# First products of a stage taken apart into those that need the rounded input and the one that needs its rest

## The reference

```python
def _ffn_half(h, g, shift, scale, gate, w_in, w_out):
    a, b = jnp.split(_modnorm(h, g, shift, scale) @ w_in, 2, axis=-1)
    return h + 0.5 * gate * ((jax.nn.silu(a) * b) @ w_out)
...
        u = rmsnorm(x, ln1_w[l])
        proj = u @ w_in[l]
...
        x = x + peer_ffn(rmsnorm(x, ln2_w[l]), peer_wq[l], peer_subkeys[l], peer_u[l], peer_v[l])
```

## Time and profile before

| | |
|---|---|
| median of 3 runs | 4942.17 us (4940.61 to 4943.07) |
| profiled execution, its own time | 4941.26 us |
| its span in the trace | 4939.4 us |
| mean granted TensorE clock | 0.937 |
| TensorE busy | 4507.5 us, 91% |
| GpSimd busy | 2803.5 us, 57% |
| ScalarE busy | 1752.6 us, 35% |
| VectorE busy | 1574.3 us, 32% |

### The profile page before, as it was taken

One profiled execution on the slowest core, in us unless ns is written; L12 is line 12 of the kernel. 1 busy time (PEld: TensorE's weight loads), 2 busy tenths in 40 slices (PEclk: granted clock), 3 DMA queues, 4 the chain that ended last, 5 costly groups with the idle time before them and its releaser, 6 DMA issues.

```text
span 4939.4 us, 72697 instructions
## 1 busy us (share of the span) xinstructions
PE 4507.5 (91%) x29978; PEld 4059.0 (82%) x29978; DVE 1574.3 (32%) x3005; ACT 1752.6 (35%) x2705; POOL 2803.5 (57%) x1354
## 2 busy tenths in 40 slices
PE   7998999999989898998867999999998866999999
PEld 5777777778878798977856999999977766999998
DVE  2211221031023232444578111112444678111112
ACT  3223322232143243441233444444441233444444
POOL 3343243344445276740467888887740467888886
PEclk9999999999999998988888999999987888999999
DMA  6624264222223144430130545545430130555544
GB/s 255 246 86 93 98 247 185 94 86 95 93 101 121 60 157 155 170 121 1 52 111 10 187 178 185 181 182 187 170 121 1 52 111 1 186 179 183 182 180 151
DMA packets 94371, 648.49 MB, mean 131 GB/s; under 512 B 9824, under 2 KB 16224, under 8 KB 16608
## 3 DMA queue, kind: packets, MB, share of 16 engines
q1 hardware_dynamic: 87120, 633.21, 34.9%
q10 hardware_dynamic: 7056, 12.49, 1.1%
HBM read 641.46 MB, written 4.19 MB: 131 GB/s over the span
## 4 chain that ended last, share of the span: by engine, by line
PE 83%; DVE 12%; ACT 2%; issue 1%; POOL 1%; DMA 1%; SPq 0%; DVEq 0%; ACTq 0%; POOLq 0%
PE ps L244 23%; PE ps L245 23%; PE ps L246 23%; PE ps L2529 3%; PE ps L399 1%; PE ps L1425 1%; PE ps L1456 1%; POOL ring_rest L260 1%; DVE arena L2091 1%; DVE x L746 1%; PE ps L1778 1%; PE ps L1825 1%; PE ps L988 1%; DMA arena<-in_mod_weights 1%; PE ps L1831 1%
## 5 line engine op out<-in xcount | busy, mean ns | idle before, releaser
L260 POOL TENSOR_TENSOR ring_rest<-ring,rounded 128x1024 fp32r<-128x1024 f32 x1032 | 2508.8, 2454 | 1621.1 <-ACT rounded L232 1353.0
L244 PE MATMUL ps<-part,rounded 128*128 128x256 f32 (+1 forms) x5760 | 1840.7, 320 | 104.5 <-DVE part L564 42.4
L245 PE MATMUL ps<-part,rounded 128*128 128x256 f32 (+1 forms) x5760 | 1828.4, 317 | 0.0
L246 PE MATMUL ps<-part,ring_rest 128*128 128x256 f32 (+1 forms) x5760 | 1826.4, 317 | 0.0
L244 PEld LDWEIGHTS ps<-part,rounded 128*128 128x128 f32 x5760 | 1112.5, 193 | 210.1 <-DVE part L564 40.7
L246 PEld LDWEIGHTS ps<-part,ring_rest 128*128 128x128 f32 x5760 | 1112.3, 193 | 69.2
L245 PEld LDWEIGHTS ps<-part,rounded 128*128 128x128 f32 x5760 | 1113.5, 193 | 66.8
L232 ACT ACTIVATE rounded<-ring 128x1024 fp32r<-128x1024 f32 x528 | 527.5, 1050 | 710.3 <-PE ps L246 702.8
L2651 ACT ACTIVATE rounded<-ring 128x1024 fp32r<-128x1024 f32 x504 | 531.5, 1055 | 378.8 <-DMA ring<-in_weights 371.7
L244 PE MATMUL ps<-x_parts,rounded 128*128 128x256 f32 x2304 | 654.9, 284 | 9.4 <-DVE x_parts L564 8.0
L245 PE MATMUL ps<-x_parts,rounded 128*128 128x256 f32 x2304 | 653.3, 284 | 0.0
(11 more groups left out here) (326 smaller groups left out, 4225.6 us busy)
## 6 DMA issues: line engine op xcount, KB each, us to landing
ring<-in_weights SPq DMA_DIRECT2D x528, 1024.0 KB, 4.8
arena<-in_mod_weights SPq DMA_DIRECT2D x72, 1024.0 KB, 7.8
arena<-bias_scratch ACTq DMA_DIRECT2D x2, 2048.0 KB, 9.2
bias_scratch<-arena ACTq DMA_DIRECT2D x1, 3072.0 KB, 32.1
x<-in_x SPq DMA_DIRECT2D x1, 2048.0 KB, 9.1
arena<-in_keys ACTq DMA_DIRECT2D x2, 1024.0 KB, 5.0
arena<-in_cst SPq DMA_DIRECT2D x1, 1216.0 KB, 29.7
arena<-in_expo ACTq DMA_DIRECT2D x1, 1024.0 KB, 5.0
```

The source lines that it names most:

```text
L244: mm(out, w[0], a[0], start=start, stop=False)
L245: mm(out, w[0], a[1], start=False, stop=False)
L246: return mm(out, w[1], a[0], start=False, stop=stop)
L260: eng.tensor_tensor(c.ring_rest[:, slot, half], c.ring[:, slot, half], c.rounded[:, (self.s0 + r) % ROUNDED, half].bitcast(F32), ALU.subtr ...
```

## The change

`product` is taken apart for the first products: `open_product` issues the two that read only the rounded input tile (w0·a0, w1·a0), `close_product` the one that reads the rest (w0·a1). For each feature tile TensorE waits for the rounded tile (`rounded_tile`, a wait on the norm's `rounded` count), issues the pairs of all open outputs, waits for the rest (`input_tile`) and issues the third products. The waits for the weights' rest stand in the first loop now, ahead of the pairs. In `PeerRoute` the bank number of the second output of block 0 moves from `part` into `first_queries`, unchanged. The sums are the same in another order.

```diff
--- before.py
+++ after.py
@@ -244,6 +244,21 @@
         mm(out, w[0], a[0], start=start, stop=False)
         mm(out, w[0], a[1], start=False, stop=False)
         return mm(out, w[1], a[0], start=False, stop=stop)
+
+    def open_product(self, out, w, a, start):
+
+        mm = self.nc.tensor.matmul
+        mm(out, w[0], a[0], start=start, stop=False)
+        mm(out, w[1], a[0], start=False, stop=False)
+
+    def close_product(self, out, w, a, stop):
+
+        return self.nc.tensor.matmul(out, w[0], a[1], start=False, stop=stop)
+
+    def rounded_tile(self, pe, k):
+
+        ready = self.before.rounded
+        pe.wait_ge(ready.sem, ready.at((k + 1) * self.before.t // N))
 
     def input_tile(self, pe, k):
 
@@ -630,12 +645,16 @@
             return last
 
         for k in range(KD // 2):
+            self.rounded_tile(pe, k)
+            outs = [(j, half, [w[:, half * KD + k, :] for w in self.weights(j)]) for j in range(2) for half in range(2)]
+            a = [u[:, k, :] for u in self.u]
+            for j, half, w in outs:
+                if k == 0:
+                    pe.wait_ge(c.rest_done[half], self.split_count(j))
+                self.open_product(c.ps[:, 2 * j + half, 0:self.t], w, a, k == 0)
             self.input_tile(pe, k)
-            for j in range(2):
-                for half in range(2):
-                    if k == 0:
-                        pe.wait_ge(c.rest_done[half], self.split_count(j))
-                    part(j, half, [k])
+            for j, half, w in outs:
+                self.close_product(c.ps[:, 2 * j + half, 0:self.t], w, a, False)
         for k in range(KD // 2, KD):
             self.input_tile(pe, k)
         for j in range(2):
@@ -1249,12 +1268,17 @@
             return last
 
         for k in range(KD // 2):
+            self.rounded_tile(pe, k)
+            outs = [(j, e, ps[:, self.bank(j, e), e * N:(e + 1) * N], [w[:, e * KD + k, :] for w in self.weights(j)])
+                    for j in range(2) for e in range(2)]
+            a = [u[:, k, :] for u in self.u]
+            for j, e, out, w in outs:
+                if k == 0:
+                    pe.wait_ge(c.rest_done[e], self.split_count(j))
+                self.open_product(out, w, a, k == 0)
             self.input_tile(pe, k)
-            for j in range(2):
-                for e in range(2):
-                    if k == 0:
-                        pe.wait_ge(c.rest_done[e], self.split_count(j))
-                    part(j, e, [k])
+            for j, e, out, w in outs:
+                self.close_product(out, w, a, False)
         for k in range(KD // 2, KD):
             self.input_tile(pe, k)
         for j in range(2):
@@ -2298,17 +2322,22 @@
             whi, wlo = self.weights(j)
             for k in tiles:
                 i = e * KD + k
-                last = self.product(ps[:, 3 if j == 0 and e else j % 2, e * N:(e + 1) * N], (whi[:, i, :], wlo[:, i, :]),
+                last = self.product(ps[:, j % 2, e * N:(e + 1) * N], (whi[:, i, :], wlo[:, i, :]),
                                     [z[:, k, :] for z in self.z], k == 0, k == KD - 1)
             return last
 
         def first_queries():
             for k in range(KD):
-                self.input_tile(pe, k)
-                for e in range(2):
+                self.rounded_tile(pe, k)
+                outs = [(e, ps[:, 3 * e, e * N:(e + 1) * N], [w[:, e * KD + k, :] for w in self.weights(0)]) for e in range(2)]
+                a = [z[:, k, :] for z in self.z]
+                for e, out, w in outs:
                     if k == 0:
                         pe.wait_ge(self.chip.rest_done[e], self.split_count(0))
-                    last = part(0, e, [k])
+                    self.open_product(out, w, a, k == 0)
+                self.input_tile(pe, k)
+                for e, out, w in outs:
+                    last = self.close_product(out, w, a, k == KD - 1)
             last.then_inc(self.chip.block_done, 1)
 
         def queries(j):
```

## The result

| | before | changed |
|---|---|---|
| median | 4941.49 us | 4951.08 us |
| runs, lowest to highest | 20, 4936.96 to 4943.32 | 20, 4947.58 to 4953.02 |
| ratio, 95% interval | | 1.0020 (1.0013 to 1.0026) |
| profiled execution, its span | 4941.26, 4939.4 us | 4947.58, 4945.8 us |

The change costs 9.6 us. The prediction said 4939.6 and a range to 4945: it was wrong, by 11.5 us, and the measured time lies 6.1 us above the range. The slowest run of before and the fastest run of the changed kernel are 4.3 us apart, so this isn't scatter. The profiled execution of the changed kernel is the fastest of its 20 runs: its trace accounts for 6.4 us of span, and what the other runs have more wasn't traced.

The account below looks back on a forecast made before the run. TensorE, busy 91% of the span, was taken as the bound, through its standstills and lower clock level. -2.64 - 1.38 + 1.50 = -2.52 us gave 4938.7 for the profiled execution, 4939.6 us as median; range 4935 to 4945.

Parts of the forecast that it names:

- Earlier starts: Three 512-token FeedForwardIn starts 0.88 us earlier each, two PeerRoute starts 0.69 us each: -2.64 and -1.38 us.
- The second block's wait: 256-token FeedForwardIn and both ProjectIn: late GpSimd weight rest leaves three third products behind the wait, 0.5 us each, 1.5 lost.
- Rises stay put or come early: Clock rises after cold starts: unmoved, gains halve, 4941.2 us, chance 0.24; or one spell sooner, 4937.5 us, chance 0.11.
- Exposed weight loads: Eight changed stages: new order needs one more 193 ns load for each of 128 products, +24.7 us, 4966.9; chance 0.01.
- What carries through: Stages behind the changed starts: the chain moves as a whole, so gains persist; in PeerRoute 0.69 us stays.
- The range: 4935 to 4945 us: early rises with one 3.3 us slow spell gained, to the slower case with one lost.
- something unseen: Leftover case without a named place or size; chance 0.02.
- The rival on the other side: 256-token FeedForwardIn and ProjectIn: longer idling and late products cost more than the starts bring, +1.2 us, 4943.3; chance 0.12.

Follow-up runs that it names:

- five-starts kernel: Kernel before with the new product order only in the three 512-token FeedForwardIn and two PeerRoute stages, the rest old; 4937.68 us, ratio 0.9998.
- the 2.2 us delay: Kernel before, none of the change, with two extra VectorE copies in Replace between the two networks; 4950.73 us, ratio 1.002.
- The filled waits alone: Kernel before with 33 unread matmul calls added in each Attention, ahead of three TensorE waits for the softmax; 4936.89 us, ratio 0.9993.

## Why the prediction was wrong, point by point

- **Earlier starts.** Right at the start itself. 0.88 us was predicted at 512 tokens, the waits shrank by 0.91; 0.69 was predicted in PeerRoute and measured. No wait stands between pairs and third products, and nothing else held the five stages. But of PeerRoute's 0.69 us little "stays": in the five-starts kernel the shift goes from -5.10 to -5.79 at the first start, is -5.48 some 5 us further on and -5.30 behind the wait for the ranking. Over three traces and both layers 0.06 to 0.26 us are left of each 0.69, so this term, taken as 1.38, was some 1 us too large.
- **The second block's wait.** Right. Three waits of "some 1.5 to 2 us" on GpSimd were forecast and are 1.52, 1.52 and 1.51 (at 1731.64 us a wait of 1.08 us for the half before stands ahead of the first, not foreseen, and without a price of its own since the last half sets the end). The price of three late products, bounded by 0.35 and 0.63 and taken as 0.5 each time, is 0.34 to 0.39 in the 256-token stage of five traces (0.02 in the changed kernel's own, where the clock rose 5.0 us behind the restart and not 5.7), 0.18 to 0.24 in the first ProjectIn of the four traces without a delay and 0.40 to 0.49 in the second: some 1.0 in place of 1.5 us.
- **Rises stay put or come early.** Both happen. At Retention (1374 us) the eight traces with the new order at 512 tokens are 4.56 to 7.05 us ahead of before (mean 5.6), and the six with the old order there between 1.83 ahead and 1.58 behind (mean 0.7 ahead): 4.9 us gained, for 2.64 predicted. In the five-starts kernel 1.3 us of it come within 6 us of the start at 566 us, where the clock rose sooner. So the sum of first-order terms was, if anything, too careful: the changed kernel reached the Attention wait 6.92 us ahead.
- **Exposed weight loads.** Rightly dismissed. The pace in the changed stages is as before, and the loss lies elsewhere.
- **What carries through.** This is the step that failed: the time that the stages behind would take was put at no change. It followed the shift through the FeedForwardIn stages and PeerRoute with the list of waits, and then said that "the chain moves as a whole". For the dependences that is so: the 0.97 us wait is 0.97 us in both traces. But the pace of TensorE behind it is not the same: in the traces, 6.9 us ahead at this wait became 6.4 us of loss at the end, by Attention (+6.6 and -6.6 us) and Rwkv (+6.5 and +6.8), which the change doesn't touch. The views I read, list waits, and a clock that falls makes no wait. I read the granted clock only where the change acts, and never in Attention and Rwkv, where it stood at 0.77 over 155 us of each layer and at 0.71 in one stretch of Attention.
- **The range.** It rested on "a slow spell of 3.3 us (1.7 us in time)" gained or lost per later cold start, as if these were small and independent. Attention's steps are 6.6 us, Rwkv's up to 6.9, there are four of them, and most kernels take the same ones in all their runs. The case that came is the forecast's "something unseen", which had a chance of 0.02. From the clocks before of these four stretches (1.00, 0.77, 0.71, 0.77) a reader could have had both ends: layer 1 of Attention at 23.33 us and layer 0 at 16.77 for one program text was in the trace from the start.
- **The rival on the other side** named the right place (256-token FeedForwardIn and ProjectIn) and the right sign with too small a price: it let those stages cost 1.2 us in their own time. Alone, they make 10.9 us, by setting off the stages behind.

**Shown**: a pure delay of 0.45 us makes a loss larger than the change's; a delay on the changed kernel makes it faster; with six unread calls in one short wait the clock stays up where it had fallen, and the loss is gone. **Open**: why Rwkv goes the one way or the other (the rows with filled waits and that for the 2.2 us delay have steps of other sizes), and which of the edits of some 0.35 us each is the decisive one, since without ProjectIn three of nine runs escape, and without both small stages eight of ten.

## What to carry to other kernels

Before a sub-microsecond edit on TensorE is priced by its own stage, read the granted clock of every later stretch, and where one program text runs at two lengths in two layers, take their difference as a unit by which any shift may pay or cost. Beside such an edit measure a control that only delays the old kernel by as much: if the control moves the time as far as the edit does, neither result is a verdict on the edit. Make the fragile stretches insensitive first (a short wait filled with unread matmuls that are no longer than the wait, counted in the trace, if its own measurement bears it out), and judge edits after that: against the kernel before on the same chip, the five starts stood at -3.2 us without it (4937.68 to 4940.92), with a fifth of the runs 8 us above, and with it at -10.3 (4929.97 to 4940.25). The filled waits alone make -4.2 (4936.89 to 4941.08). Only the -10.3 is clear of no change by its interval.

## What was unexpected about the hardware

- A wait of TensorE of 0.97 us, in otherwise busy work, can bring the granted clock down: from the wait on, 23.34 us at 0.71 against 16.77 at 1.00 for the same instructions. Whether it does turned on hundredths of a microsecond in its place, and there are two edges: lost between 19.99 and 20.46 us behind the last rise, kept at 19.96 and less and at 20.56 and more, with the fall at 20.48.
- A delay doesn't keep its distance to the clock's changes: 0.45 us of delay at 1951 us were some 0.05 us against them at 2215 us. The work falls into step with the clock's changes, so most kernels' runs agree on the side they take and give a steady median, which looks like a property of the code.
- TensorE can be busy without a gap and stay at the lower level, as in this stretch of Rwkv in the kernel before:

```profile
2297.00:2319.00 22.00, 22.00 (x107) 20.88 (x106) 10.37 (x23) 0.00 (x0) 0.00 (x0) 0.50 0.00 1
```

- The Trainium skill (same page and section as above) says that for modelling the ramp's cost is under 1% of a typical kernel's span, and advises against fitting a count of slow matmuls. Here the lower level as a whole costs more than that: a mean granted clock of 0.937 is 6.3% below 1.00 (at most that share of the span, since some of it falls on waits). The 13.0 us that a delay of 0.45 us moved are 0.26% of the span, but for judging a change of 0.05% they are the larger number by far.
